# Down-projection weight loads moved from SyncE's DMA queue to ScalarE's, in a 16-expert MoE layer on one core

## The chip, the cores and the metric

The kernel runs on one core of one Trainium2 chip. The metric is the device time of one execution in microseconds (us): median 1182.03 us of 3 runs, from 1181.91 to 1183.86. The core has five engines that run side by side, each with its own list of instructions: TensorE (PE; PEld is its weight load), VectorE (DVE), ScalarE (ACT), GpSimd (POOL) and SyncE (SP, which only starts transfers). They wait for one another, and for transfers (DMAs), through semaphores. A DMA that an engine starts goes into that engine's queue; 16 DMA engines carry out what lies in the queues. In the trace, q1 (hardware_dynamic) is the queue of SyncE's transfers and q0 (software_dynamic) that of GpSimd's.

## What is computed

An encoder layer on two sequences (256 and 512 tokens, width 1024, float32): input norm, a mixer of attention and a state-space scan, an output projection and a norm, then an expert-choice mixture of 16 experts, a gated embedding and a last norm. The change touches the experts alone:

```python
def _expert_choice(h, w_router, w_gate, w_up, w_down):
    n_tok, d = h.shape
    cap = CAPACITY_FACTOR * n_tok // N_EXPERTS
    aff = jax.nn.softmax((h @ w_router).astype(jnp.float32), axis=-1)
    gate, idx = lax.top_k(aff.T, cap)
    xe = h[idx]
    hid = jax.nn.silu(jnp.einsum("ecd,edf->ecf", xe, w_gate)) * jnp.einsum("ecd,edf->ecf", xe, w_up)
    ye = jnp.einsum("ecf,efd->ecd", hid, w_down) * gate[..., None].astype(h.dtype)
    return jnp.zeros_like(h).at[idx.reshape(-1)].add(ye.reshape(-1, d))
```

Each expert takes 32 rows of the short sequence and 64 of the long one, 96 in all. Its three weight matrices are 1024 x 1024 float32, 4 MiB each, so 12 MiB for one expert and 192 MiB for all.

## The kernel before

The parts ahead of the experts fill the first half of the time. The experts' stage then runs with PE as its backbone. For expert e PE does, in the order in which its program is written: `gate_up(e)` (line 1905; the gate and the up product together, in four quarters q of the contracted dimension), `rows_turn(e + 1)` (line 1883; transposes of the next expert's gathered rows), `down(e - 1)` (line 1917; the down product of the expert before, in two halves d), and `hid_turn(e)` (line 1891; transposes of the hidden values). The down product runs one expert behind the gate and up product, and in the last round expert 14's and 15's down products follow each other.

Weights live in single buffers. `gu_w[q]` (four of 2 MiB) holds one quarter of the gate and up weights, `dn_w[d]` (two of 2 MiB) one half of the down weights. Together they hold 12 MiB, one expert. A buffer can be loaded again once PE has finished the products that read it: `s_ug` counts finished quarters, `s_ud` finished halves. PE in turn waits for `s_guw[q]` ahead of a quarter and `s_dnw[d]` ahead of a half.

SyncE starts all of these loads. `load_gu(e, q)` (line 512) starts two DMAs of 1 MiB, whose rows are 8 KiB for each partition, and `load_dn(e, d)` (line 515) one DMA of 2 MiB, which reads rows of 4 KiB. SyncE's loop over e waits for each quarter of expert e - 1 and then loads that quarter of expert e; after the four quarters it waits for each half of `down(e - 2)` and loads that half of expert e - 1. So the loads stand in its queue in the order in which PE will use them.

GpSimd gathers the rows of an expert to come (line 659, one indirect DMA) and scatters each finished result into `acc_rows` in HBM with an add (line 681, three indirect DMAs). In the embedding's part, ahead of the experts, it stores to `acc_rows` with plain DMAs (line 665). ScalarE does two things for an expert: `silu(e)` (line 988), after all four quarters, and `rows_out(e + 1)` (line 726), which copies the transposed rows out of PSUM. VectorE multiplies (line 1408), copies the transposed hidden values (line 1402) and scales the result by the gate (line 1415).

```python
            with sp.Fori(2, NE) as e:
                for q in range(QC):
                    sp.wait_ge(s_ug, 4 * (e - 1) + q + 1)
                    load_gu(e, q)
                for d in range(2):
                    sp.wait_ge(s_ud, 2 * (e - 2) + d + 1)
                    load_dn(e - 1, d)
```

Of the kernel before, what the change touches and what calls it, by code (L numbers as in the profile page):

```python
# [28 lines left out]
P = 128  # L29
# [10 lines left out]
NE = 16  # L40
# [25 lines left out]
def hymba_layer(nc, A, consts, out_prompt, out_sample):  # L66
# [16 lines left out]
    with ctx:  # L83
# [3 lines left out]
        def sem(name):  # L87
            return ctx.enter_context(nc.semaphore(name))
# [66 lines left out]

        s0, s1 = ring[:, 0, :], ring[:, 1, :]
        NPREV = sum(n - 1 for _, n in SEQS)
        state = s0[:, 0:4 * NPREV * 256].rearrange("p (d g n c) -> p d g n c", d=2, g=2, n=NPREV)
        prob = s1[:, 0:2048].rearrange("p (b c) -> p b c", b=4)
# [49 lines left out]
        dn_w = [slot[j].rearrange("p (k c) -> p k c", k=4) for j in (5, 2)]  # L209
# [118 lines left out]
        s_dnw = [sem(f"s_dnw{d}") for d in range(2)]  # L328
        s_ug = sem("s_ug")
        s_ud = sem("s_ud")  # L330
# [102 lines left out]
        def _(sp):  # L433
# [71 lines left out]

            wg = A["w_e_gate"][0].rearrange("e (p k) f -> e p k f", p=P)
            wu = A["w_e_up"][0].rearrange("e (p k) f -> e p k f", p=P)
            wd = A["w_e_down"][0].rearrange("e (k p) f -> e p k f", p=P)

            def load_gu(e, q):  # L510
                for i, w in enumerate((wg, wu)):
                    sp.dma_start(gu_w[q][:, i], w[e, :, 2 * q:2 * q + 2, :]).then_inc(s_guw[q], 16)

            def load_dn(e, d):
                sp.dma_start(dn_w[d], wd[e, :, 4 * d:4 * d + 4, :]).then_inc(s_dnw[d], 16)

            sp.wait_ge(s_gs, NG)
            for h in range(2):
# [8 lines left out]
            sp.dma_start(gB[:], bc(A["ln2_g"][0])).then_inc(s_ln2, 16)  # L527
            sp.dma_start(bB[:], bc(A["ln2_b"][0])).then_inc(s_ln2, 16)
            sp.wait_ge(s_pg, 2 * NT)
            load_dn(0, 0)  # L530
            load_dn(0, 1)
            for q in range(QC):
                sp.wait_ge(s_ug, q + 1)
                load_gu(1, q)
            with sp.Fori(2, NE) as e:
                for q in range(QC):
                    sp.wait_ge(s_ug, 4 * (e - 1) + q + 1)
                    load_gu(e, q)
                for d in range(2):
                    sp.wait_ge(s_ud, 2 * (e - 2) + d + 1)  # L540
                    load_dn(e - 1, d)
            for d in range(2):
                sp.wait_ge(s_ud, 2 * (NE - 2) + d + 1)
                load_dn(NE - 1, d)

            sp.wait_ge(s_scat, 16 * NG3 * NE)
            for t in range(NT):
# [169 lines left out]
        def _(act):  # L717
# [7 lines left out]
            def copy(o, i):  # L725
                return nc.scalar.activation(o, i, ACT.Copy)  # L726
# [217 lines left out]
            def sigmoid(u):  # L944
                act.wait_ge(s_pg, u + 1)
                if u >= 2:
                    act.wait_ge(s_acc[u % 2], 16 * (u // 2))
                nc.scalar.activation(sig[u % 2], ps[:, 2 * (u % 2), :], ACT.Sigmoid).then_inc(s_sig, 1)
# [30 lines left out]
            def rows_out(e):  # L979
                act.wait_ge(s_xeT_p, e + 1)  # L980
                for half in range(2):
                    last = copy(xeT[:, 4 * half:4 * half + 4, :],
                                ps[:, TURN + half, 0:4 * CAP].rearrange("p (k c) -> p k c", k=4))
                last.then_inc(s_xeT, 1)

            def silu(e):
                act.wait_ge(s_ug, 4 * (e + 1))
                nc.scalar.activation(hid, ps[:, GU:GU + NG3, 0:256], ACT.Silu).then_inc(s_hs, 1)  # L988
# [2 lines left out]
                sigmoid(u)  # L991
            rows_out(0)
            sigmoid(2 * NT - 1)
            silu(0)
            rows_out(1)
            with act.Fori(1, NE - 1) as e:
                silu(e)
                rows_out(e + 1)
            silu(NE - 1)

            for t in range(NT):
                root()
# [981 lines left out]
```

## Time and profile before

| what | value |
|---|---|
| median of 3 runs | 1182.03 us (1181.91 to 1183.86) |
| the profiled execution's own time | 1182.11 us |
| its span, first to last instruction | 1180.3 us |
| PE busy | 1072.2 us, 91% of the span |
| ACT busy | 253.0 us, 21% |
| q1, SyncE's queue | 234.48 MB, 50.9% of 16 DMA engines' span |
| q0, GpSimd's queue | 18.88 MB, 6.5% |
| HBM read | 237.62 MB, mean 215 GB/s over the span |

A time in a row counts from the start of the span. Lines of the kernel are written L1905. "Idle before" is the time that an engine stood still ahead of an instruction, with what ended it. In the strips each digit stands for a slice of a fortieth of the stretch shown, and tells the busy share in tenths. Shares of busy time are averages over stages that have different limits, so stretches are read one by one.

### The profile page before, as it was taken

What the parts mean: (1) busy time and instruction counts of PE and PEld (TensorE: products, weight loads), DVE (VectorE), ACT (ScalarE), POOL (GpSimd) and SP (SyncE); (2) the same over time, 40 slices, a digit from 0 to 9 for tenths busy, and PEclk for the clock granted to TensorE, in tenths of its full rate; (3) what the DMA queues carried; (4) which work ended last, traced back from release to release, by engine and by line L of the source; (5) the groups of instructions that cost most, each with busy time, mean ns of one, the idle gap of its engine ahead of it and who ended that gap; (6) DMA issues with size and microseconds to landing.
All of it is one profiled execution on the core that took longest, in us unless ns stands there. A gap on an engine that the chain in (4) does not pass through costs nothing.

```text
span 1180.3 us, 20730 instructions
## 1 busy us (share of the span) xinstructions
PE 1072.2 (91%) x8811; PEld 611.9 (52%) x8811; DVE 439.7 (37%) x870; ACT 253.0 (21%) x530; POOL 287.5 (24%) x311
## 2 busy tenths in 40 slices
PE   5999778888998899999999999999999999999940
PEld 3568666665655587866643344444443344444420
DVE  5436785457678867656100011111011011111018
ACT  1143334256656621300011000000000000000002
POOL 0006994234545100000100122211122122210134
PEclk9999988979999999789999999999999999999985
DMA  9010200300000620404269999999999999999854
GB/s 337 14 61 11 72 1 1 98 10 0 2 1 1 211 101 36 187 18 158 97 252 406 385 385 386 398 396 386 388 397 392 390 388 387 397 393 404 320 166 176
DMA packets 63119, 254.01 MB, mean 215 GB/s; under 512 B 7384, under 2 KB 15448, under 8 KB 46688
## 3 DMA queue, kind: packets, MB, share of 16 engines
q1 hardware_dynamic: 52544, 234.48, 50.9%
q0 software_dynamic: 10528, 18.88, 6.5%
q8 instruction: 32, 0.52, 0.2%
q14 instruction: 15, 0.12, 0.0%
HBM read 237.62 MB, written 15.73 MB: 215 GB/s over the span
## 4 chain that ended last, share of the span: by engine, by line
PE 72%; DVE 11%; DMA 7%; POOL 6%; ACT 2%; issue 2%; SPq 0%; DVEq 0%; POOLq 0%; ACTq 0%
PE ps L1905 25%; PE ps L1917 12%; PE ps L1563 4%; DMA ring<-in_w_e_up 2%; DMA late<-in_w_e_down 2%; PE ps L1669 2%; PE ps L1684 2%; PE ps L1805 2%; PE ps L1557 2%; PE ps L1807 2%; PE ps L1806 2%; PE ps L1811 2%; PE ps L1883 1%; PE ps L1774 1%; PE ps L1775 1%
## 5 line engine op out<-in xcount | busy, mean ns | idle before, releaser
L1905 PE MATMUL ps<-ring,mix 128*32 128x512 f32 x1536 | 170.7, 592 | 1.1 <-DMA ring<-in_w_e_up 1.1
L1905 PE MATMUL ps<-late,mix 128*32 128x512 f32 x1536 | 171.1, 593 | 0.0
L1408 DVE TENSOR_TENSOR mix<-mix,ps 128x768 f32<-128x768 f32 x16 | 15.3, 954 | 321.6 <-ACT mix L988 321.6
L988 ACT ACTIVATE mix<-ps 128x768 f32<-128x768 f32 x16 | 13.0, 811 | 478.8 <-PE ps L1905 478.8
L1905 PEld LDWEIGHTS ps<-ring,mix 128*32 128x32 f32 x1536 | 49.7, 110 | 116.5 <-issue 113.4
L1905 PEld LDWEIGHTS ps<-late,mix 128*32 128x32 f32 x1536 | 48.2, 110 | 108.7 <-issue 107.8
L1917 PE MATMUL ps<-late,mix 128*32 128x256 f32 x1536 | 86.2, 380 | 2.9 <-DVE mix L1402 2.5
L1917 PE MATMUL ps<-ring,mix 128*32 128x256 f32 x1536 | 85.9, 379 | 1.4 <-DMA ring<-in_w_e_down 1.4
L1415 DVE TENSOR_SCALAR mix<-ps,att 128x256 f32<-128x256 f32 x48 | 20.3, 477 | 162.0 <-PE ps L1917 162.0
L681 POOL DMA_INDIRECT acc_rows<-mix,idx_now x48 | 74.9, 1561 | 20.5 <-POOL idx_now L689 10.7
L1917 PEld LDWEIGHTS ps<-ring,mix 128*32 128x32 f32 x1536 | 49.7, 110 | 34.6 <-DMA ring<-in_w_e_down 1.9
L1917 PEld LDWEIGHTS ps<-late,mix 128*32 128x32 f32 x1536 | 48.9, 110 | 35.2 <-DVE mix L1402 3.0
L686 POOL COPY idx_now<-idxT 96x1 int32 (+1 forms) x14 | 2.5, 181 | 219.2 <-PE ps L1883 219.2
L689 POOL COPY idx_now<-idx 128x3 int32 (+1 forms) x16 | 3.0, 186 | 195.3 <-DVE mix L1415 195.3
L1646 PE MATMUL ps<-xT 128*128 128x512 f32 (+1 forms) x96 | 45.0, 555 | 1.3 <-issue 1.3
L1563 PE MATMUL ps<-ring,xT 128*128 128x512 f32 x96 | 44.9, 623 | 1.2 <-ACT xT L726 1.2
L1537 PE MATMUL ps<-xl,wh 128*128 128x512 f32 (+1 forms) x128 | 44.0, 344 | 0.0
L850 ACT ACTIVATE ring<-ps,att 128x512 f32<-128x512 f32 (+1 forms) x48 | 29.3, 611 | 49.0 <-DVE att L1182 48.8
L1091 DVE SCALAR_TENSOR_TENSOR late<-late,cw 128x770 f32<-128x770 f32 x32 | 39.1, 1226 | 0.9
L1805 PE MATMUL ps<-ring_r,xT_r 128*128 128x512 f32 x96 | 39.3, 409 | 0.0
L1660 PE MATMUL ps<-cst,ring 128*128 128x128 f32 x160 | 27.9, 291 | 11.4 <-DVE gb_in L1190 5.4
L1806 PE MATMUL ps<-late_r,xT_r 128*128 128x512 f32 x96 | 37.9, 395 | 0.0
(289 smaller groups left out, 1812.4 us busy)
## 6 DMA issues: line engine op xcount, KB each, us to landing
late<-in_w_e_gate SPq DMA_DIRECT2D x32, 1024.0 KB, 18.0
late<-in_w_e_up SPq DMA_DIRECT2D x32, 1024.0 KB, 20.0
ring<-in_w_e_gate SPq DMA_DIRECT2D x32, 1024.0 KB, 17.0
ring<-in_w_e_up SPq DMA_DIRECT2D x32, 1024.0 KB, 20.0
late<-in_w_e_down SPq DMA_DIRECT2D x16, 2048.0 KB
ring<-in_w_e_down SPq DMA_DIRECT2D x16, 2048.0 KB
ring<-in_w_in SPq DMA_DIRECT2D x3, 2048.0 KB, 9.0
late<-in_w_ple_gate SPq DMA_DIRECT2D x2, 2048.0 KB, 14.1
```

What stands on the lines that cost most here:

```text
L681: pool.indirect_dma_start(acc_quarters, bass.IndirectOffsetOnAxis(ap=idx_now[:, 1 + i:2 + i], axis=0), ye[:, i, :], None, compute_op=ALU.a ...
L850: nc.scalar.activation(prob[:, u % 4, 0:L], ps[:, u % 3, 0:L], ACT.Exp, bias=att[:, 0, u:u + 1], scale=HD ** -0.5, accum_out=att[:, 1, u:u ...
L1091: ins = nc.vector.scalar_tensor_tensor(conv[:, m, :], u_pad[:, m, j:j + CW], cw[:, m, j:j + 1], conv[:, m, :], ALU.mult, ALU.add)
L1537: nc.tensor.matmul(o, w_h, xl[:, k, a * P:(a + w) * P], start=False, stop=False)
L1557: last = nc.tensor.matmul(bank[:, 0:272], lhs[k], wkv[:, k, :], start=(k == 0), stop=(k == KD - 1))
L1563: last = nc.tensor.matmul(bank, lhs[k], slotk[0][:, k, :], start=(k == 0), stop=(k == KD - 1))
L1646: nc.tensor.matmul(ps[:, u % 3, 0:n * P], qT[:, h % 4, t * P:(t + 1) * P], kz[:, h // 4, a * P:(a + n) * P], start=True, stop=True).then_i ...
L1660: last = nc.tensor.transpose(ps[:, 3, b * P:(b + 1) * P], prob[:, u % 4, b * P:(b + 1) * P], ident)
L1805: nc.tensor.matmul(ps[:, b, :], x_h, wpg_h[h][:, k, :], start=False, stop=False)
L1806: nc.tensor.matmul(ps[:, b, :], x_h, wpg_l[h][:, k, :], start=False, stop=False)
L1905: last = nc.tensor.matmul(ps[32 * j:32 * (j + 1), GU + g, :].rearrange("p (w c) -> p w c", w=2), xeT[:, k, 32 * g:32 * (g + 1)], gu_w[q][: ...
L1917: last = nc.tensor.matmul(ps[32 * j:32 * (j + 1), DN + g, 0:256], src[:, k, 32 * g:32 * (g + 1)], dn_w[d][:, i, 256 * j:256 * (j + 1)], st ...
```

## The change

`load_dn` and its waits leave SyncE's program and go into ScalarE's. Expert 0's two halves are loaded after the last `sigmoid`. The loop over experts starts at 2 rather than 1 (expert 1's `silu` and expert 2's `rows_out` are written out ahead of it), and each round first waits for the two halves of `down(e - 2)`, starting the load of that half of expert e - 1 after each, and then goes on with `silu(e)` and `rows_out(e + 1)`. The last two experts' loads stand behind the loop, ahead of and behind the last `silu`. Buffers, semaphores, sizes and what each load waits for stay as they are. SyncE keeps the gate and up loads.

```diff
@@ SyncE's program
-            def load_dn(e, d):
-                sp.dma_start(dn_w[d], wd[e, :, 4 * d:4 * d + 4, :]).then_inc(s_dnw[d], 16)
...
             sp.wait_ge(s_pg, 2 * NT)
-            load_dn(0, 0)
-            load_dn(0, 1)
             for q in range(QC):
                 sp.wait_ge(s_ug, q + 1)
                 load_gu(1, q)
...
                 for q in range(QC):
                     sp.wait_ge(s_ug, 4 * (e - 1) + q + 1)
                     load_gu(e, q)
-                for d in range(2):
-                    sp.wait_ge(s_ud, 2 * (e - 2) + d + 1)
-                    load_dn(e - 1, d)
-            for d in range(2):
-                sp.wait_ge(s_ud, 2 * (NE - 2) + d + 1)
-                load_dn(NE - 1, d)
@@ ScalarE's program
             rows_out(0)
             sigmoid(2 * NT - 1)
+            def load_dn(e, d):
+                act.dma_start(dn_w[d], wd[e, :, 4 * d:4 * d + 4, :]).then_inc(s_dnw[d], 16)
+
+            load_dn(0, 0)
+            load_dn(0, 1)
             silu(0)
             rows_out(1)
-            with act.Fori(1, NE - 1) as e:
+            silu(1)
+            rows_out(2)
+            with act.Fori(2, NE - 1) as e:
+                for d in range(2):
+                    act.wait_ge(s_ud, 2 * (e - 2) + d + 1)
+                    load_dn(e - 1, d)
                 silu(e)
                 rows_out(e + 1)
+            for d in range(2):
+                act.wait_ge(s_ud, 2 * (NE - 3) + d + 1)
+                load_dn(NE - 2, d)
             silu(NE - 1)
+            for d in range(2):
+                act.wait_ge(s_ud, 2 * (NE - 2) + d + 1)
+                load_dn(NE - 1, d)
```

## Rows read from the trace of the kernel before

**Rows 1.** Page, part 2: the span in 40 equal slices of 29.5 us.
```profile
PE   5999778888998899999999999999999999999940
DMA  9010200300000620404269999999999999999854
GB/s 337 14 61 11 72 1 1 98 10 0 2 1 1 211 101 36 187 18 158 97 252 406 385 385 386 398 396 386 388 397 392 390 388 387 397 393 404 320 166 176
```

**Rows 2.** Chain that ended last: start us, us, what.
```profile
823.61 20.74 PE ps L1905 x192
844.35 1.06 PE ps L1883 x8
845.41 10.50 PE ps L1917 x192
855.91 0.81 PE ps L1891 x6
856.71 20.74 PE ps L1905 x192
...
1043.74 28.39 DMA ring<-in_w_e_up
```

**Rows 3.** Busy time by stretch: stretch, its us, engines' busy us, PEclk, DMA share, GB/s.
```profile
823.61:856.71 33.10, 33.10 (x403) 13.88 (x406) 3.15 (x7) 1.68 (x3) 6.01 (x6) 1.00 1.03 392
989.11:1022.21 33.10, 33.10 (x403) 13.88 (x406) 3.15 (x7) 1.68 (x3) 6.01 (x6) 1.00 1.03 390
1022.21:1055.48 33.27, 33.27 (x403) 13.78 (x406) 3.15 (x7) 1.68 (x3) 6.01 (x6) 1.00 1.03 391
1055.48:1089.89 34.41, 33.33 (x402) 13.66 (x406) 3.15 (x7) 1.68 (x3) 4.87 (x4) 1.00 1.03 405
```

**Rows 4.** DMA issues of 691:725, then of 989:1023: last number is us to landing.
```profile
late<-in_w_e_gate SPq DMA_DIRECT2D x2, 1024.0 KB, 12.9
late<-in_w_e_up SPq DMA_DIRECT2D x2, 1024.0 KB, 16.3
...
late<-in_w_e_gate SPq DMA_DIRECT2D x2, 1024.0 KB, 23.4
late<-in_w_e_up SPq DMA_DIRECT2D x2, 1024.0 KB, 25.3
```

**Rows 5.** Waits of 1022:1138: us in total, times, longest.
```profile
PE ps L1905 <- DMA ring<-in_w_e_up: 1.1, 1, 1.1
PE ps L1917 <- DMA ring<-in_w_e_down: 1.4, 1, 1.4
PE ps L1917 <- DMA late<-in_w_e_down: 0.4, 1, 0.4
```

**Rows 6.** Timeline of 845:862 and of ACT and SP at 844: start, us, instruction.
```profile
844.42 0.81 ACT L988 ACTIVATE mix<-ps 128x768 f32<-128x768 f32 x1 [31.20 <-PE ps L1905]
844.97 0.38 SPq L512 DMA_DIRECT2D ring<-in_w_e_up  x1
850.93 0.38 SPq L515 DMA_DIRECT2D late<-in_w_e_down  x1
856.10 0.38 SPq L515 DMA_DIRECT2D ring<-in_w_e_down  x1
862.20 0.35 SPq L512 DMA_DIRECT2D late<-in_w_e_gate  x1
```

**Rows 7.** SyncE's longest issue (timeline of SP).
```profile
1060.97 7.63 SPq L512 DMA_DIRECT2D late<-in_w_e_gate  x1
```

**Rows 8.** DMA of 921:929, gate and up alone, then of 938:942, down alone.
```profile
DMA packets 465, 3.38 MB, mean 422 GB/s; under 512 B 53, under 2 KB 53, under 8 KB 53
...
DMA packets 425, 1.68 MB, mean 421 GB/s; under 512 B 14, under 2 KB 14, under 8 KB 425
```

**Rows 9.** DMA of 555.2:557, gate and up beside stores of line 665.
```profile
DMA packets 138, 0.75 MB, mean 416 GB/s; under 512 B 19, under 2 KB 19, under 8 KB 74
q1 hardware_dynamic: 80, 0.52, 70.1%
q0 software_dynamic: 58, 0.23, 30.5%
```

**Rows 10.** DMA of 950.2:953.2, gate and up beside a gather of line 659.
```profile
DMA packets 168, 0.97 MB, mean 322 GB/s; under 512 B 10, under 2 KB 10, under 8 KB 90
q1 hardware_dynamic: 88, 0.64, 68.7%
q0 software_dynamic: 80, 0.33, 35.3%
```

**Rows 11.** DMA issues of 440:600 (idle queues), then a gather of 989:1023.
```profile
late<-in_w_e_gate SPq DMA_DIRECT2D x2, 1024.0 KB, 4.8
mix<-x_rows,idx_now POOLq DMA_INDIRECT x2, 4.2
...
mix<-x_rows,idx_now POOLq DMA_INDIRECT x1, 8.8
```

More of the change, by code:

```diff
@@ L507, in _ @@
             wu = A["w_e_up"][0].rearrange("e (p k) f -> e p k f", p=P)
-            wd = A["w_e_down"][0].rearrange("e (k p) f -> e p k f", p=P)
             def load_gu(e, q):
@@ L993, in _ @@
             sigmoid(2 * NT - 1)
+            wd = A["w_e_down"][0].rearrange("e (k p) f -> e p k f", p=P)
+            def load_dn(e, d):
+                act.dma_start(dn_w[d], wd[e, :, 4 * d:4 * d + 4, :]).then_inc(s_dnw[d], 16)
+            load_dn(0, 0)
+            load_dn(0, 1)
             silu(0)
             rows_out(1)
-            with act.Fori(1, NE - 1) as e:
+            silu(1)
[4 more added lines that the diff above has]
+                    load_dn(e - 1, d)
                 silu(e)
                 rows_out(e + 1)
+            for d in range(2):
+                act.wait_ge(s_ud, 2 * (NE - 3) + d + 1)
+                load_dn(NE - 2, d)
             silu(NE - 1)
+            for d in range(2):
+                act.wait_ge(s_ud, 2 * (NE - 2) + d + 1)
+                load_dn(NE - 1, d)
             for t in range(NT):
```

## The prediction

> **What bounds the kernel now.** I read the page's slices first. From slice 21 to 36 PE is busy in nine tenths or more, and so are the DMA engines, at 385 to 406 GB/s [rows 1]. That is the experts' stage, from about 601 us on; nothing ahead of it is changed, save that expert 0's down loads start after one more activation. Two limits lie close together there, so the stage's own cycles decide.
>
> The chain of waits shows PE's cycle. One expert is 20.74 + 1.06 + 10.50 + 0.81 us, back to back: 33.1 us [rows 2], and the table by stretch has PE busy in all of it [rows 3]. The DMA engines' cycle shows in the landings. A load of gate weights took 12.9 us from issue to landing around 700 us and 23.4 around 1000; one of up weights went from 16.3 to 25.3 [rows 4]. Those stretches are nine experts apart, so the transfers fall behind by (10.5 + 9.0) / 2 / 9 = 1.1 us per expert. **The DMA cycle is therefore 34.2 us**, and the stage is bound by transfers. It doesn't show as PE waits because of a reserve: a quarter's buffer is used again 33.1 us after it was last used, and its product takes a quarter of 20.74, 5.2, so a load has 33.1 - 5.2 = 27.9 us. Landings reach that only in the last rounds (28.39 us [rows 2]). PE's cycles there are 33.27 and 34.41 us, 0.17 and 1.31 too long [rows 3], and then two halves of a down product wait 0.4 and 1.4 [rows 5]. **PE waits about 3.3 us for weights in the whole stage.** A change of order alone can't give back more.
>
> **What of the order.** SyncE's queue holds the loads in the order in which PE uses them: four quarters, two down halves, four quarters. So all of the lag falls evenly on every load, and the whole reserve is used before any load is late.
>
> **The change, part by part.** *Removed from SyncE:* 32 starts of 2 MiB, at 0.38 us [rows 6]. SyncE waits for PE between its loads, and its longest start, 7.63 us [rows 7], only stands at the end of transfers that are already queued. Worth 0 us; at most the gate load behind such a start would be queued some us sooner, into a queue that is full.
>
> *Added to ScalarE:* 32 starts and their waits. The trace has no DMA start on ScalarE. Its price is bounded below by 0 (it takes nothing that another engine does in time) and above by SyncE's longest, 7.63 us; I take SyncE's usual 0.38, the nearest, since the queue will hold two loads at most. Cover: ScalarE stands idle for 31.20 us ahead of each `silu` [rows 6]. The starts fall at the end of the two halves, 850.93 and 856.10, and the next `silu` is due one cycle after 844.42, at 877.5: 21 us later. Two starts of even 7.63 us fit. Without that cover each us would hold up `silu`, the hidden values and PE in every expert. The new waits can't hold up anything either: behind them stand `silu(e)` and `rows_out(e + 1)`, which need `gate_up(e)`, which PE does after `down(e - 2)`. Sum 0.
>
> *Moved:* 64 MiB out of an ordered queue into one of its own. How do two queues share? Beside stores of GpSimd's queue, 138 - 74 = 64 gate and up packets of 8 KiB went with 74 - 19 = 55 packets of 4 KiB [rows 9]; beside a gather it was 168 - 90 = 78 against 90 - 10 = 80 [rows 10]. And a gather lands in 8.8 us where SyncE's loads take 23 to 25, against 4.2 with idle queues [rows 4, 11]: it passes SyncE's backlog instead of standing behind it. So the queues take turns packet by packet. The down loads are packets of 4 KiB (all 425 of a stretch of down alone are under 8 KB [rows 8]), the gate and up loads of 8. **While both queues hold work the down loads get one byte in three.**
>
> A down pair of 4.19 MB then draws 8.39 MB of gate and up with it, which is just the gate and up weights of one expert. With GpSimd's traffic in between that is a whole DMA cycle, 34.2 us, and an unloaded load shows what comes on top: 1.05 MB land in 4.8 us [rows 11], of which 2.5 are transfer at 422 GB/s [rows 8], so 2.3. Together 36.5 us. The time at hand runs from the end of a first half (its load is started, 850.93) to the beginning of the second half of the next expert, 33.1 us later. **At worst the pair's second load is 36.5 - 33.1 = 3.4 us late**, while gate and up loads lie ready early. That is the new wait, at line 1917.
>
> It comes only while SyncE's queue doesn't run dry in a cycle. SyncE starts nothing between 844.97 and 862.20 [rows 6]. In that gap the down loads, started at 850.93 and 856.10, can have the engines to themselves, if the gate and up backlog at 850.93 is small. They have 11.3 us until 862.20 and need 10.0 (4.19 MB at 421 GB/s [rows 8]). With a backlog of g us about g - 1.3 are left over, and some 3 us of scatter are served between. From then on they get a third of the time, and 20 us are left, so g - 1.3 + 3 must stay under 6.6: g under 5. Today's up load takes 16.3 us to land around 700 us [rows 4]; 6 us have gone by when the down load starts, 2.3 are no transfer and 3 are the scatter that is counted already, so g is 5 there, among the loads of expert 4, with 1.1 more or less per expert. I put the onset at expert 4. As bounds I take expert 2 (without the scatter's share g passes 5 there) and expert 9, five experts of lag later.
>
> After the onset PE can't draw on the reserve any more and follows the DMA cycle: it loses 1.1 us per expert on average, in waits of up to 3.4 at every second or third expert. From expert 4 to 14 that is 11 x 1.1 = 12.1. The first late pair overshoots by 0 to 3.4, I take 1.7. The waits of the last down half, 1.4, stay, since the last two loads have the engines almost alone. So 15.2 us of waits take the place of 3.3: **+11.9 us**. Bounds: onset at 9 without overshoot, 6 x 1.1 + 1.4 - 3.3 = +4.7; onset at 2 with all of it, 13 x 1.1 + 3.4 + 1.4 - 3.3 = +15.8.
>
> *The price of taking turns itself* is open. No row has two loads of 128 partitions side by side. Stores beside loads move 416 GB/s against 422 [rows 8, 9]: nothing that can be told from none. A gather beside loads moves 322, a quarter less [rows 10]; it writes SBUF like the down loads, but 96 partitions and single rows picked by an index. I take the stores' value, 0, because the down loads spread over the partitions as the gate and up loads do, and keep the gather's for a rival.
>
> At one place the Trainium skill bears on this. The trace shows about equal counts of packets in turns. The page "DMA: Bandwidth & Descriptors", section "Queues, rings and completion order", has a DMA engine drain a whole packet of some 9 to 17 descriptors from one queue before it goes to the next. Turns of equal length in descriptors leave one byte in three and my sum; turns long enough to take all of a gate load but half of a down load would be the second rival's case. No row here shows the length of a turn on ScalarE's queue.
>
> **Sum.** The profiled execution took 1182.11 us, 1.8 of them outside its span of 1180.3, which the change doesn't touch; the median of the runs is 1182.03, the same within 0.1. 1182.1 + 11.9 = **1194.0 us**.
>
> **Rivals.** *No change.* The bytes are the same and the DMA engines are never idle until the last loads, so they run dry at the same time as now; if PE's work left at that point is also the same, so is the time: 1182.1. For it: the cycle of 34.2 us. Against it: with loads out of order PE has more left when the queue runs dry. The Trainium skill, on the same page "DMA: Bandwidth & Descriptors", section "Issuing engines are not separate DMA queues", says that starting DMAs on several engines only saves the time it takes to start them; SyncE's starts lie on no path here, so by that rule the time stays too.
>
> *Faster.* If ScalarE's queue gets half of the bytes or more, the pair lands in 2 x 10.0 + 4 + 2.3 = 26 us, inside 33.1, and the gate and up loads no longer have 10 us of down loads ahead of them. Then the waits of 3.3 us go: 1178.8. It decides once the down loads get over about two bytes in five. For it speaks only that the length of a turn isn't seen; against it the counts [rows 9, 10].
>
> *Dear turns.* If loads of two queues disturb each other as the gather does, 12.58 MB take 39 us instead of 29.9, a cycle of 43.5: 10.4 over PE's for 14 experts, less up to 15 of reserve: +130, some 1310 us. A quarter of that loss gives about 1220.
>
> **How the numbers follow.** Forecast (1186 to 1205) 0.61; no change 0.13; faster 0.08; dear turns 0.18, of which a third lies under 1222. Two thirds of that last and little else lie outside, so the range goes from 1178.5, the faster case, to 1222. Some 0.2% is what a measurement of this kernel can tell from no change (2.4 us): faster 0.07, same 0.14, slower 0.79.
>
> **What would show it.** Right: waits of line 1917 for in_w_e_down of 2 to 4 us at some experts from the fourth to the sixth on; gate and up landings that stay under about 20 us rather than climb to 28; the DMA engines idle for some 10 us more in the last rounds; as many 4 KiB packets as 8 KiB ones while both queues hold work. Wrong: waits at line 1905 instead (turns favour ScalarE), a rate well under 390 GB/s in the stage (turns are dear), or `silu` held up by a start on ScalarE.

## The result and the profile after

The changed kernel takes 1189.76 us (median of 5 runs, 1188.98 to 1191.35) against 1181.91 for the kernel before: a ratio of 1.0067, 95% interval 1.0053 to 1.0082. It is 7.9 us slower, where 11.9 were forecast (1194.0, range 1178.5 to 1222). The profiled execution took 1189.76 us, too, with a span of 1187.9.

All of it lies in the experts' stage. From the first gate and up product to the end of the last down product the kernel before needs 535.9 us (601.3 to 1137.2) and the changed one 543.9 (601.1 to 1145.0); what follows takes 43 us in both. Line numbers moved: gate and up products are L1911 now, down products L1923, `silu` L976 and the start of a down load L985.

The waits for weights in the stage (us in total, times, longest), first of PE's products, then of its weight load:

```profile
PE ps L1923 <- DMA ring<-in_w_e_down: 10.4, 6, 1.9
...
PEld ps L1923 <- DMA ring<-in_w_e_down: 13.3, 6, 2.4
```

They are the only waits for weights. The gate and up product, where the kernel before lost 1.5 of its 3.3 us (0.17 and 1.31 [rows 3]), doesn't wait once. The timeline of PE shows the six, each at the second half of a down product (four of them here):

```profile
786.09 5.39 PE L1923 MATMUL ps<-ring,mix 128*32 128x256 f32 x96 [1.75 <-DMA ring<-in_w_e_down]
854.10 5.39 PE L1923 MATMUL ps<-ring,mix 128*32 128x256 f32 x96 [1.60 <-DMA ring<-in_w_e_down]
922.20 5.39 PE L1923 MATMUL ps<-ring,mix 128*32 128x256 f32 x96 [1.70 <-DMA ring<-in_w_e_down]
...
1139.57 5.39 PE L1923 MATMUL ps<-ring,mix 128*32 128x256 f32 x96 [1.90 <-DMA ring<-in_w_e_down]
```

786.09 is expert 4's second half, then come 6, 8, 10, 12 and, at the end, 15. In the table by stretch (columns as in [rows 3]) two cycles together now take 68.1 us instead of 66.2, at 393 to 394 GB/s, where the kernel before has 390 to 392:

```profile
757.20:792.28 35.08, 33.33 (x403) 13.80 (x406) 3.17 (x7) 1.68 (x3) 6.01 (x6) 1.00 1.03 394
792.28:860.29 68.01, 66.41 (x800) 27.66 (x804) 6.30 (x13) 3.37 (x6) 12.03 (x12) 1.00 1.03 394
860.29:928.39 68.10, 66.40 (x800) 27.65 (x804) 6.29 (x13) 3.37 (x6) 12.03 (x12) 1.00 1.03 393
...
1097.72:1145.01 47.29, 42.81 (x582) 18.88 (x582) 4.81 (x10) 2.09 (x2) 9.73 (x8) 1.00 0.60 204
```

The last stretch runs from the last gate and up product to the end. In the kernel before the same stretch reads:

```profile
1089.89:1137.30 47.41, 43.02 (x583) 19.40 (x582) 4.82 (x10) 2.09 (x2) 9.73 (x8) 1.00 0.81 288
```

Busy shares of 0.60 of 47.29 and 0.81 of 47.41 us make 28.4 and 38.4 us. Over the whole span the DMA engines move the same bytes, but they stand idle 10 us longer at the end: they are done early, and PE still has work left.

The DMA issues of 823:857 (last number: us to landing) show whose loads are late. Gate and up loads land in 12 to 21 us, where the kernel before ended at 23 to 25 [rows 4]; the second down half needs 29:

```profile
ring<-in_w_e_down ACTq DMA_DIRECT2D x1, 2048.0 KB, 29.3
late<-in_w_e_gate SPq DMA_DIRECT2D x2, 1024.0 KB, 12.2
late<-in_w_e_up SPq DMA_DIRECT2D x2, 1024.0 KB, 15.6
ring<-in_w_e_gate SPq DMA_DIRECT2D x2, 1024.0 KB, 17.7
ring<-in_w_e_up SPq DMA_DIRECT2D x2, 1024.0 KB, 21.3
late<-in_w_e_down ACTq DMA_DIRECT2D x1, 2048.0 KB, 17.5
```

How the queues share is seen in 738:745, where SyncE's (q1) and ScalarE's (q10) hold work throughout and GpSimd's (q0) up to about 742:

```profile
DMA packets 579, 2.84 MB, mean 406 GB/s; under 512 B 37, under 2 KB 132, under 8 KB 356
q1 hardware_dynamic: 240, 1.83, 63.0%
q10 hardware_dynamic: 228, 0.92, 31.8%
q0 software_dynamic: 111, 0.10, 8.7%
```

579 - 356 = 223 packets of 8 KiB (gate and up) went against 356 - 132 = 224 of 4 KiB (down). That is packet for packet, and so 1.83 MB against 0.92: of these two queues' bytes, the down loads get one in three. ScalarE itself loses nothing by it. Its starts take 0.39 us, and its next `silu` still comes after 31.20 us of idle time, as in the kernel before [rows 6]:

```profile
751.44 0.39 ACTq L985 DMA_DIRECT2D late<-in_w_e_down  x1
756.61 0.39 ACTq L985 DMA_DIRECT2D ring<-in_w_e_down  x1
778.02 0.81 ACT L976 ACTIVATE mix<-ps 128x768 f32<-128x768 f32 x1 [31.20 <-PE ps L1911]
```

### The profile page after: what moved, and what is told of

Same layout as the page of the kernel before. It is cut to its first block, busy times and chain, and to the rows that moved or that the text cites. A ratio compares the mean times of both kernels' runs of the same rounds, so it can differ in the third digit from the quotient of the medians.

```text
span 1187.9 us, 20723 instructions
## 1 busy us (share of the span) xinstructions
PE 1073.5 (90%) x8811; PEld 613.6 (52%) x8811; DVE 439.8 (37%) x870; ACT 253.0 (21%) x530; POOL 287.6 (24%) x311
## 4 chain that ended last, share of the span: by engine, by line
PE 64%; DMA 15%; DVE 11%; POOL 6%; ACT 2%; issue 2%; SPq 0%; ACTq 0%; DVEq 0%; POOLq 0%
PE ps L1911 19%; DMA ring<-in_w_e_down 13%; PE ps L1923 12%; PE ps L1569 4%; PE ps L1675 2%; PE ps L1811 2%; PE ps L1690 2%; PE ps L1563 2%; PE ps L1812 2%; PE ps L1813 2%; PE ps L1817 2%; PE ps L1780 1%; PE ps L1781 1%; PE ps L1782 1%; DVE xT L1462 1%
## 5 line engine op out<-in xcount | busy, mean ns | idle before, releaser
L1911 PE MATMUL ps<-late,mix 128*32 128x512 f32 x1536 | 171.0, 593 | 0.0
L1911 PE MATMUL ps<-ring,mix 128*32 128x512 f32 x1536 | 170.6, 592 | 0.0
L976 ACT ACTIVATE mix<-ps 128x768 f32<-128x768 f32 x16 | 13.0, 811 | 486.4 <-PE ps L1911 486.4
L1911 PEld LDWEIGHTS ps<-ring,mix 128*32 128x32 f32 x1536 | 49.9, 110 | 114.9 <-issue 114.9
L1911 PEld LDWEIGHTS ps<-late,mix 128*32 128x32 f32 x1536 | 48.3, 110 | 108.6 <-issue 108.6
L1923 PE MATMUL ps<-ring,mix 128*32 128x256 f32 x1536 | 86.0, 379 | 10.4 <-DMA ring<-in_w_e_down 10.4
L1923 PE MATMUL ps<-late,mix 128*32 128x256 f32 x1536 | 86.2, 380 | 2.5 <-DVE mix L1408 2.5
L1923 PEld LDWEIGHTS ps<-ring,mix 128*32 128x32 f32 x1536 | 49.2, 110 | 45.2 <-DMA ring<-in_w_e_down 13.3
L1923 PEld LDWEIGHTS ps<-late,mix 128*32 128x32 f32 x1536 | 48.4, 110 | 35.1 <-DVE mix L1408 3.0
L1812 PE MATMUL ps<-late_r,xT_r 128*128 128x512 f32 x96 | 38.4, 400 | 0.0
L1813 PE MATMUL ps<-ring_r,mix_r 128*128 128x512 f32 x96 | 38.4, 400 | 0.0
```

Source lines behind the costliest of these rows:

```text
L1812: nc.tensor.matmul(ps[:, b, :], x_h, wpg_l[h][:, k, :], start=False, stop=False)
L1813: nc.tensor.matmul(ps[:, b, :], x_l, wpg_h[h][:, k, :], start=False, stop=(k == KD - 1))
L1911: last = nc.tensor.matmul(ps[32 * j:32 * (j + 1), GU + g, :].rearrange("p (w c) -> p w c", w=2), xeT[:, k, 32 * g:32 * (g + 1)], gu_w[q][: ...
L1923: last = nc.tensor.matmul(ps[32 * j:32 * (j + 1), DN + g, 0:256], src[:, k, 32 * g:32 * (g + 1)], dn_w[d][:, i, 256 * j:256 * (j + 1)], st ...
```

## Experiments

The theory: queues take turns by packets, so loads in a queue of their own come out of the order of use, in a stage whose transfers fall behind by about 1 us per expert. Its rivals: ScalarE is a bad starter, or two queues side by side cost rate. All ratios are to the kernel before, run on the same chip at the same time; a number in brackets behind a ratio is its 95% interval. The experiments are called runs 1 to 8 below. Their code is shown in parts; "..." stands for what is left out.

**1. Down weights in rows of 8 KiB, on ScalarE's queue.** This changes the share and leaves queue, starter and bytes alone.

```diff
-wd = A["w_e_down"][0].rearrange("e (k p) f -> e p k f", p=P)
+wd = A["w_e_down"][0].rearrange("e (j p b) f -> e p j (b f)", p=P, b=2)
...
-                                                   hid[:, i, b * P:(b + 1) * P], ident)
+                                                   hid[:, i, b:256:2], ident)
```

> The changed kernel, but the down weights are read in rows of 8 KiB instead of 4 (a partition takes two neighbouring rows of the matrix, and the transposes of the hidden values pick columns to match). Same bytes, same queue, same starter. Theory (queues take turns packet by packet, so the down loads get their share by packet size): one byte in two instead of one in three, a pair of down loads lands about 26 us after its first start instead of 34.7, the five waits of 1.9 us at the second half disappear, and the time comes to 1179 to 1182 us. Rival (ScalarE's starts or its queue are slow in themselves): the waits stay and the time is 1188 to 1191. Rival (turns between two queues cost rate): also 1188 to 1191.

Measured: 1184.3 us, 1.0029 (1.0018 to 1.0040), so of the 7.9 us 5.5 come back by the medians and 4.5 by the ratios; the time lies between the theory's and the rivals'. The waits at the second half do go, but for the last one. In 823:857 the second half now lands in 20.4 us. The waits for weights of its PE:

```profile
PE ps L1911 <- DMA ring<-in_w_e_up: 2.2, 2, 1.5
PE ps L1923 <- DMA ring<-in_w_e_down: 1.6, 1, 1.6
```

The share is confirmed: row length alone moved the load from 29 to 20 us, and in 832:834, with both queues full, they moved 0.38 and 0.39 MB (49 and 47 packets). What was missed is that the down loads now take their bytes from the gate and up loads, which are needed first; so these are late instead, at two of the last rounds. PE's cycle also grew by 0.11 us, to 33.21, since its transposes now pick every second column.

**2. The same rows on SyncE's queue**, the partner of 1, built on the kernel before.

> The kernel before with down weights read in rows of 8 KiB; all loads stay in SyncE's queue. It is the partner of the run with wide rows on ScalarE's queue. Theory: no share is decided by packet size in a single queue, so the gain is only what larger packets save themselves, 0 to 0.3 us per expert of lag; at best the 3.3 us of waits go: 1178.5 to 1182. If instead wide rows speed up loads as such by much, this one gains as much as the partner does (8 us): 1174.

Measured: 1181.37 us, 1.0001 (0.9988 to 1.0013). As expected, wide rows don't gain 8 us by themselves. PE waits for weights once, 1.2 us at the last half; its cycle is 33.21 us here, too. Between 1 and 2 only the queue differs, and it costs 2.9 us.

**3. Only the first half on ScalarE's queue.** SyncE loads the second half at its old place. Against the changed kernel:

```diff
 @@ SyncE's loop, after the four quarters
+                sp.wait_ge(s_ud, 2 * (e - 2) + 2)
+                load_dn(e - 1, 1)
...
 @@ ScalarE's loop
-                for d in range(2):
+                for d in range(1):
...
```

> One part of the change alone: only the first half of the down weights is loaded through ScalarE's queue, the second half goes back to its old place in SyncE's. Theory (one byte in three while both queues hold work): ScalarE's queue now holds 2.1 MB at a time, draws 4.2 MB of SyncE's with it and lands in about 20 us, inside the 27.9 at hand; the second half stands in order. So no wait before the last rounds, and 1179 to 1184 us. Rival (the turns or ScalarE's starts cost by themselves, in proportion to the loads moved): half of the loss, 1185 to 1187.

Measured: 1185.62 us, 1.0044 (1.0028 to 1.0061). The theory's number is missed, and the rival's, half of the loss, is met. The timeline tells what happened. The down halves land in time but for the last; the last quarter of the gate and up product is late in six rounds, one after the other, from 903.78 on:

```profile
903.78 5.36 PE L1919 MATMUL ps<-ring,mix 128*32 128x512 f32 x48 [0.57 <-DMA ring<-in_w_e_up]
937.90 5.36 PE L1919 MATMUL ps<-ring,mix 128*32 128x512 f32 x48 [0.81 <-DMA ring<-in_w_e_up]
971.91 5.36 PE L1919 MATMUL ps<-ring,mix 128*32 128x512 f32 x48 [0.70 <-DMA ring<-in_w_e_up]
```

Every cycle is 33.1 us up to there and 34.0 from there on (903.78 to 937.90 and on to 971.91 are 34.12 and 34.01). A price in proportion to the loads moved would make this DMA cycle shorter than that of the changed kernel, where twice as much is moved. It is the same, 34.0 against 34.05, at 393 GB/s in both; only the point from which it rules is later. So the half on ScalarE's queue passes the quarter that stands ahead of it in the order of use. I had only asked whether the down half lands in time, not whom it passes.

**4. Queues exchanged:** ScalarE starts the gate and up loads of experts 1 to 15, SyncE the down loads. Against the kernel before:

```diff
 @@ ScalarE's loop
             with act.Fori(1, NE - 1) as e:
+                for q in range(QC):
+                    act.wait_ge(s_ug, 4 * e + q + 1)
+                    load_gu(e + 1, q)
                 silu(e)
...
```

> The queues exchanged: ScalarE starts the gate and up loads of experts 1 to 15, SyncE the down loads, with the same waits. Theory (only the two packet sizes matter, not who starts): the same waits of 1.6 to 2 us at the second half of every second expert from the fifth on, 1188 to 1192 us. Rival (the loss comes from ScalarE as the starter of the late loads): the second halves, now SyncE's, land in time, and if anything gate and up loads are late: waits at the gate and up product, not at the second half.

Measured: 1193.22 us, 1.0102 (1.0083 to 1.0121). Some 3.7 us of it are a fault of the exchange: ScalarE's first `silu` comes after its starts, PE stands still for 3.09 us once, and its next product takes 6.73 instead of 5.36 us at a mean granted clock of 0.78; the first two cycles take 26.01 and 34.47 us instead of 23.64 and 33.10. The rest, 7.6 us, is of the size of the changed kernel's loss. The loads that are late are again those of the second down half, though SyncE starts them:

```profile
823.65 5.39 PE L1924 MATMUL ps<-ring,mix 128*32 128x256 f32 x96 [0.50 <-DMA ring<-in_w_e_down]
...
925.66 5.39 PE L1924 MATMUL ps<-ring,mix 128*32 128x256 f32 x96 [0.20 <-DMA ring<-in_w_e_down]
960.34 5.39 PE L1924 MATMUL ps<-ring,mix 128*32 128x256 f32 x96 [1.37 <-DMA ring<-in_w_e_down]
```

They come less regularly than expected (0.2 to 3.8 us; the profile is of the slowest execution, 1196.42 us), and the first is at expert 5 rather than 4. But they come at the same product, with the starters exchanged. ScalarE as the starter is out.

**5. No lag: both kernels without the scatters** and the waits for them.

```diff
                 for i in range(NG3):
-                    pool.indirect_dma_start(acc_quarters, ...
+                    pass
...
```

> The kernel before without the scatters of the experts' results (they are left out, with the waits for them; the output then lacks the experts' part). That takes about 2.8 us of transfers out of each DMA cycle: 34.1 becomes some 31.3, under PE's 33.1. Theory: transfers don't fall behind any more, PE waits for weights only in the last round, and behind it the last scatter's 8 us are gone as well: 1168 to 1174 us.

> The changed kernel without the scatters, partner of the run of the kernel before without them. Theory (the loss is the reserve that the lag can't draw on any more): without lag there is nothing to draw, all down loads land in under 30 us, and the two partners differ by less than 1.5 us. Rival (two queues cost rate, or ScalarE starts loads late): the changed one stays about 8 us behind its partner.

Measured: 1170.72 us for the kernel before and 1170.88 for the changed one (ratios 0.9911, 0.9895 to 0.9928, and 0.9903, 0.9887 to 0.9920). The stages take 533.4 and 533.6 us. Each waits for weights once, in the last round, 1.0 and 1.2 us. In 958:992 the second half lands in 9.6 us on SyncE's queue and in 9.7 on ScalarE's:

```profile
ring<-in_w_e_down SPq DMA_DIRECT2D x1, 2048.0 KB, 9.6
```
```profile
ring<-in_w_e_down ACTq DMA_DIRECT2D x1, 2048.0 KB, 9.7
```

The transfers don't fall behind here: second halves take 18.4 us to land around 660 in the changed order, and 9.5 around 1040. Then the two orders cost the same, 0.2 us apart. A price that PE would pay directly, for two queues or for ScalarE as a starter, would be seen here. A small price on the transfers could hide in their slack; it is excluded by the full queues, with 393 GB/s for two and 391 for one. **The loss needs the lag.** (The scatters go out together with the lag; no run takes out one without the other.)

**6. Wide rows without the cost on PE, on ScalarE's queue.** `silu` and the product after it write the hidden values with the even columns first, and the transposes read neighbours again.

```diff
-nc.scalar.activation(hid, ps[:, GU:GU + NG3, 0:256], ACT.Silu)
+nc.scalar.activation(hid.rearrange("p i (b c) -> p i b c", b=2),
+                     ps[:, GU:GU + NG3, 0:256].rearrange("p i (c b) -> p i b c", b=2), ACT.Silu)
...
```

> The changed kernel with down weights in rows of 8 KiB, as before, but the picking of columns for it is done where ScalarE and VectorE write the hidden values, so that PE's transposes read neighbouring columns again (they had become 0.11 us longer per expert). Theory (after the run with wide rows: the down loads land in time, and what is left of its loss are these 1.7 us on PE and gate and up loads that wait for turns): stage shorter by 1.5 to 2 us than with the picking on PE, 1182 to 1183.5 us. If the rest of the loss were a price of turns, spread over all experts, nothing of it would be seen as waits for weights.

Measured: 1184.98 us, 1.0029 (1.0017 to 1.0042). The stage of the profiled execution is 1.5 us shorter than in 1 (536.9 against 538.4), as expected, but the median is not; the two can't be told apart by their times. The waits are at the gate and up product again, four of them:

```profile
PE ps L1911 <- DMA ring<-in_w_e_up: 2.4, 4, 1.2
PE ps L1923 <- DMA ring<-in_w_e_down: 1.2, 1, 1.2
```

**7. The same on SyncE's queue.**

> The kernel before with wide rows and the same cheap picking; all loads in SyncE's queue, in the order of use. Theory: the lag falls by some 0.3 us per expert, no quarter waits, only the last half does (1.2 us): 1179 to 1181 us, 2 to 3 less than its partner on ScalarE's queue.

Measured: 1180.86 us, 0.9987 (0.9973 to 1.0001), 4.1 less than its partner. All cycles are 33.1 us but for the first, as in all runs; no quarter waits. The expected wait of 1.2 us at the last half isn't in the trace, for another reason: the product before it took 7.07 instead of 5.39 us, at a mean granted clock of 0.75, after PE had stood still for 2.53 us.

**8. And the last expert's down weights into gate and up buffers** that are free by then.

```diff
             for d in range(2):
-                sp.wait_ge(s_ud, 2 * (NE - 2) + d + 1)
-                load_dn(NE - 1, d)
+                sp.wait_ge(s_ug, 4 * (NE - 1) + d + 1)
+                sp.dma_start(dn_last[d].rearrange("p (j b) f -> p j (b f)", b=2),
+                             wd[NE - 1, :, 2 * d:2 * d + 2, :]).then_inc(s_guw[d], 16)
...
```

> The same on SyncE's queue, and the last expert's down weights go into two gate and up buffers that are free by then, so that they don't wait for the down product before. Theory: the last wait of 1.2 to 1.4 us goes as well: 1177.5 to 1180 us, under both the kernel before and the changed one. What is then left of PE's idle time in the last round are 2.5 us that it waits for VectorE's copy.

Measured: 1179.59 us, 0.9979 (0.9967 to 0.9992): under both kernels, by 2.5 and 10.2 us in the medians. By the times it can't be told apart from 7. PE waits for no weights in the stage (532.2 us); what is left in the last round is

```profile
PE ps L1924 <- DVE mix L1404: 2.5, 1, 2.5
```

## Why the prediction was right, and which terms were off

**The mechanism held.** Where the wait would appear (the second down half), that it would come in lumps at every second or third expert, that gate and up loads would be early, that the engines would be idle 10 us more at the end, and that starts on ScalarE would hide: each is in the rows above. The turns cost nothing that can be seen: 393 GB/s in the stage's cycles against 390 to 392 [rows 3]. So the *dear turns* are out, as are *no change* and *faster*, which wanted an even end or a larger share.

**The size was off by a third, in three terms.** The lag: 1.1 us per expert over 11 experts was 12.1; measured are five waits that lengthen their cycles by 1.8 to 2.0 us, 9.5 together, so 0.95 per expert over ten experts, 4 to 13. I read the lag from landings of loads, which rose by 1.0 (up) and 1.17 (gate), and took the mean; the cycle itself came out at 68.1 / 2 = 34.05 us, not 34.2. The eleventh expert, 14, isn't late: no gate and up loads stand behind its own, and its second half lands in 16.0 us instead of 26 to 29. The overshoot of the first late pair, taken as 1.7, is 0. And the last wait is 1.9 instead of 1.4. Together 9.5 + 1.9 = 11.4 us of waits in place of 3.3: +8.1, and +7.9 measured.

The overshoot was sized by a worst case that assumed gate and up loads always pending: 36.5 us from the pair's first start to its landing. Measured is 786.04 - 751.44 = 34.6. SyncE's queue does run dry for a moment: in 764.5 to 766 it moves 7 packets and ScalarE's 101. That the whole difference of 1.9 us comes from there is not shown. The waits come at every second expert, because one wait of 1.9 pays for two cycles' lag of 0.95.

**The onset was hit in part by luck.** The prediction let the wait come only while SyncE's queue doesn't run dry in a cycle; it did run dry, and the wait came. And it let the backlog grow by the lag, 1.1 us per expert, for which it gave expert 4 with bounds from 2 to 9. What filled the reserve was faster: the second halves of experts 1 to 4 land in 21.8, 23.9, 26.6 and 29.4 us, 2.1 to 2.8 more each time, two to three times the lag. From the start of such a load to its product there are 27.5 us (723.51 to 751.05), so the fourth is late by 1.9. A queue with a third of the bytes would take up the lag threefold; that this is the reason is argued, not shown.

Two figures of the prediction don't follow from its own sums, and neither moves the 1194.0: the bounds of the forecast, +4.7 and +15.8, give 1187 to 1198, not 1205; and a quarter of the loss of 130 us gives 1215, not 1220.

**One rule behind most of the runs.** As long as no load is late PE goes at 33.1 us per expert, and from the first late load on at about the DMA cycle: 34.05 us on average in the changed kernel, 34.0 in run 3, 33.8 in the two late cycles of the kernel before and 33.7 in run 6. The splits tried here bring that point forward. It lies at 1038 us in the kernel before, at 939 in run 6, at 904 in run 3 and at 786 in the changed kernel, and the stages take 535.9, 536.9, 539.3 and 543.9 us, in the same order. Runs 1 and 4 don't stand in this row: their PE loses time of its own (0.11 us per cycle, 3.7 us at the start). This also tells what the prediction's *faster* rival lacked: a share of one half does land the down loads in time, as it said, but takes the time from gate and up loads (runs 1 and 6), and the stage is still not faster than before.

On the Trainium skill's rule, "DMA: Bandwidth & Descriptors", section "Issuing engines are not separate DMA queues": transfers of all starters share the same 16 engines and starting from several saves only the starts. The traces agree on the rate. They don't agree with the reading that the time then stays: 0.67% were lost, by the order. In the same page's section "Queues, rings and completion order" an engine takes some 9 to 17 descriptors of a queue in a turn; 223 packets met 224 here, which fits turns of any equal length, and no run shows how long one is.

## What to carry to other kernels

When transfers are the slower side and buffers are single, one queue that holds the loads in the order of use did better than each split tried here (runs 2 and 7 against 1 and 6); a second queue added no rate, it let later loads pass earlier ones. If loads must be split, the share goes by packet size (4 KiB beside 8 KiB gave one byte in three, 8 beside 8 one in two), so rows of equal length belong on both sides, and the question to ask of each moved load is not only when it lands but which load it passes. Compare the cycle of the transfers with that of the engine first: where the transfers kept up with PE instead of falling behind by 0.95 us per expert (run 5), the same move cost nothing.

## What the runs showed that was not expected

The share between two queues of plain loads is exact: 223 packets to 224 in 7 us, with a third queue at work beside them for part of the time. And two such queues side by side lose no rate, 392 to 394 GB/s in full cycles, although a gather beside loads moves only 322 [rows 10]; what slows the gather's neighbours was not tried. And PE's granted clock fell to a mean of 0.75 of full speed for one product after the same wait of 2.53 us in runs 4 and 7 (7.07 us), but stayed at 1.00 in both kernels and in run 8 (5.39 us); what decides is open.
